# A diffusion trunk on one core: both panels' weights ahead of each modulation chunk, the last chunk directly behind the third on TensorE, and the high part ahead of silu in tile 0

## The reference

```python
def rms_norm(x, g):
    y = x * lax.rsqrt(jnp.mean(x * x, axis=-1, keepdims=True) + RMS_EPS)
    return y * g

def modulate(h, shift, scale):
    return h * (1.0 + scale) + shift

def swiglu(h, w_gu, w_down):                      # D_FF = 2816
    u = h @ w_gu
    return (jax.nn.silu(u[..., :D_FF]) * u[..., D_FF:]) @ w_down

for i in range(DEPTH):                            # DEPTH = 2, N_MOD = 9
    mx = (jax.nn.silu(c) @ ada_w[i] + ada_b[i]).reshape(B, 1, N_MOD, D_MODEL)
    mc = (jax.nn.silu(c_ctx) @ ada_w[i] + ada_b[i]).reshape(N_MOD, D_MODEL)
    x = x + 0.5 * mx[:, :, 2] * swiglu(modulate(rms_norm(x, norm_g[i, 0]), mx[:, :, 0], mx[:, :, 1]),
                                       ffn_w_gu[i, 0], ffn_w_down[i, 0])
    ...                                           # the same for ctx with mc
    # then a mixer (pooling and attention in layer 0, a recurrent block in layer 1), then a second swiglu
```

## Time and profile before

| | |
|---|---|
| median of 3 runs | 2848.53 us (2847.98 to 2848.59) |
| the profiled execution | 2844.29 us, span 2842.5 us |
| PE busy | 2685.2 us (94% of the span) |
| PE weight load busy | 2498.1 us (88%) |
| DVE, POOL, ACT busy | 1461.2, 905.6, 784.8 us |
| mean clock granted to PE | 0.975 of full |
| HBM read | 252.70 MB, 90 GB/s over the span |

### The profile page before, as it was taken

How to read it: one execution, slowest core, us unless ns; L and a number is a source line. 1 busy time by engine, 2 the same in 40 slices (tenths; PEclk the granted TensorE clock), 3 DMA queues, 4 the chain that set the end, 5 groups by cost and what they waited for, 6 DMA issues and landing times.

```text
span 2842.5 us, 40073 instructions
## 1 busy us (share of the span) xinstructions
PE 2685.2 (94%) x15151; PEld 2498.1 (88%) x15151; DVE 1461.2 (51%) x2479; ACT 784.8 (28%) x1053; POOL 905.6 (32%) x367
## 2 busy tenths in 40 slices
PE   6899999999989899999999999999998886899998
PEld 4899999998957899999998999999997775778887
DVE  5565456565363656556657324322248886432233
ACT  3222122222164322111122221111125664332222
POOL 0422233222322232322232232232324443344442
PEclk9999999999999999999999999999999998999999
DMA  5444344423300244434442223322211112233332
GB/s 202 119 118 132 97 118 118 132 75 79 108 27 27 70 118 118 137 93 118 118 136 57 59 59 96 89 61 64 68 46 52 56 52 58 68 94 99 89 104 80
DMA packets 413089, 256.87 MB, mean 90 GB/s; under 512 B 6653, under 2 KB 405846, under 8 KB 413014
## 3 DMA queue, kind: packets, MB, share of 16 engines
q1 hardware_dynamic: 413014, 255.87, 31.2%
HBM read 252.70 MB, written 4.25 MB: 90 GB/s over the span
## 4 chain that ended last, share of the span: by engine, by line
PE 51%; issue 29%; DVE 8%; POOL 7%; ACT 4%; DMA 0%; POOLq 0%; SPq 0%; DVEq 0%; ACTq 0%
PE pair_b L1696 24%; PE pair_a L1696 22%; POOL w_lo L711 7%; DVE ada_sums L1127 1%; DVE decay L1656 1%; DVE decay L1654 1%; DVE h_lo L1278 1%; DVE gate_i L1650 1%; DVE root L1648 1%; ACT decay L1065 1%; ACT root L1067 1%; PE pair_r L2051 1%; PE pair_c L2033 1%; PE pair_c L1778 1%; PE pair_a L1686 0%
## 5 line engine op out<-in xcount | busy, mean ns | idle before, releaser
L711 POOL TENSOR_TENSOR w_lo<-raw,w_hi 128x1024 fp32r<-128x1024 f32 (+3 forms) x302 | 837.4, 2774 | 1733.4 <-ACT w_hi L821 1733.4
L821 ACT ACTIVATE w_hi<-raw 128x1024 fp32r<-128x1024 f32 (+3 forms) x302 | 337.6, 1118 | 1279.3 <-PE pair_b L1696 440.6
L1167 DVE TENSOR_TENSOR work_g<-work_s,pair_b 128x768 f32<-128x768 f32 (+1 forms) x88 | 78.1, 888 | 680.9 <-PE pair_b L1696 518.2
L1127 DVE SCALAR_TENSOR_TENSOR ada_sums<-ada_raw,cvec,ada_sums 128x256 f32<-128x256 f32 x896 | 404.5, 524 | 0.0
L1696 PE MATMUL pair_a<-h_hi,w_hi 128*128 128x384 f32 x1312 | 340.6, 340 | 17.6 <-POOL w_lo L711 17.4
L1696 PE MATMUL pair_a<-h_lo,w_hi 128*128 128x384 f32 x1312 | 335.1, 336 | 0.0
L1696 PE MATMUL pair_a<-h_hi,w_lo 128*128 128x384 f32 x1312 | 334.4, 335 | 0.0
L1696 PE MATMUL pair_b<-h_hi,w_hi 128*128 128x384 f32 x1168 | 298.3, 336 | 8.4 <-POOL w_lo L711 8.4
L1696 PE MATMUL pair_b<-h_hi,w_lo 128*128 128x384 f32 x1168 | 297.5, 335 | 0.0
L1696 PE MATMUL pair_b<-h_lo,w_hi 128*128 128x384 f32 x1168 | 297.3, 335 | 0.0
L1696 PEld LDWEIGHTS pair_a<-h_hi,w_hi 128*128 128x128 f32 x1312 | 234.6, 189 | 30.0 <-issue 16.3
(11 more groups left out here) (290 smaller groups left out, 4330.7 us busy)
## 6 DMA issues: line engine op xcount, KB each, us to landing
raw<-in_ffn_w_gu_dram SPq DMA_DIRECT2D x176, 512.0 KB, 4.0
ada_raw<-in_ada_w_dram SPq DMA_DIRECT2D x64, 1024.0 KB, 5.2
raw<-in_ffn_w_down_dram SPq DMA_DIRECT2D x64, 704.0 KB, 5.5
raw<-in_rg_w_in_dram SPq DMA_DIRECT2D x20, 512.0 KB, 3.7
ada_first<-in_ada_w_dram SPq DMA_DIRECT2D x4, 2048.0 KB, 13.5
raw<-in_ab_w_in_dram SPq DMA_DIRECT2D x16, 512.0 KB, 3.9
raw<-in_rg_w_out_dram SPq DMA_DIRECT2D x8, 640.0 KB, 4.4
raw<-in_ab_w_out_dram SPq DMA_DIRECT2D x8, 512.0 KB, 4.1
```

What stands on the lines that cost most here:

```text
L711: nc.gpsimd.tensor_tensor(wl[:, par, 0:kt * P], raw[:, par, 0:kt * P], wh[:, par, 0:kt * P].bitcast(F32), ALU.subtract).then_inc(split_rea ...
L821: nc.scalar.activation(wh[:, par, 0:kt * P], raw[:, par, 0:kt * P], ACT.Copy).then_inc(hi_done, 1)
L1127: step = nc.vector.scalar_tensor_tensor(out=sums[v], in0=tiles(k), scalar=c_k, in1=sums[v], op0=ALU.mult, op1=ALU.add)
L1167: nc.vector.tensor_tensor(gbuf[:, 0, 0:W], sbuf[:, 0, 0:W], up, ALU.mult)\
```

## The change

Three edits. First, SP issues the loads of both panels of a tile, or of a pair of down panels, and the modulation chunk behind them. Second, PE runs `ada_rows(1)` directly behind `turn_ada(2)`, ahead of the first tile, and `turn_ada(3)` behind the first of the eight pieces. Third, in tile 0 of gu00 ACT rounds the next even panel before it takes silu; for this the tile is taken out of the loop.

```diff
                     def gate_up(i, between):
                         load(i * 2 + p0, 0, KD, gu[:, :, span(i * P + h * KC * P, P)])
+                        load(i * 2 + (p0 + 1), 1, KD, gu[:, :, span(i * P + (DFF + h * KC * P), P)])
                         between()
-                        load(i * 2 + (p0 + 1), 1, KD, gu[:, :, span(i * P + (DFF + h * KC * P), P)])
...
                         for r in range(2):
                             load(i * 2 + (p0 + r), r, KC, dn[:, h * KC:(h + 1) * KC, span(i * (2 * P) + r * P, P)])
-                            if r == 0:
-                                between()
+                        between()
...
                 p0, F0 = first[f"gu{f}{h}"], GU_BEFORE[f, h]
-                with act.Fori(0, KC - 1) as i:
+                if p0 == 0:
+
+                    for r in range(2):
+                        act.wait_ge(panel_used, r + 1)
+                        high(2 + r)
+                        if r == 0:
+                            silu(F0, p0)
+                with act.Fori(int(p0 == 0), KC - 1) as i:
                     silu(i + F0, i * 2 + p0)
...
             turn_ada(2, KD + 4)
+            ada_rows(1, pC[:, 512:1024])
 
             def modulation_ends(k0, half, r):
 
-                if (k0, half, r) == (0, 0, 1):
-                    ada_rows(1, pC[:, 512:1024])
-                elif (k0, half, r) == (0, 1, 0):
+                if (k0, half, r) == (0, 0, 0):
                     turn_ada(3, 4).then_inc(ada_used, 1)
```

## The result

The changed kernel takes **2823.51 us** (median of 4 runs, 2822.25 to 2825.37) against 2848.56 us for the kernel before (median of 4, 2847.98 to 2849.76). The ratio is 0.9912 with a 95% interval of 0.9895 to 0.9929.

A forecast was written before the change was run, and what follows sets the result against it. PE, busy 94% of the span, was taken as the bound, with gains from its idle time and the lower clock behind it. 5.3 + 0 + 4.9 + 2.9 + 4.8 = 17.9 us, so 2848.53 - 17.9 = 2830.6 us; range 2824 to 2838.

The forecast's parts named there:

- The last chunk and the opening: Ahead of tile 0 of gu00: the moved chunk makes the turn begin earlier, winning 5.3 us (4.1 to 7.1).
- The stop in tile 1 stays: Ahead of `pair_a` in gu00: POOL gets in behind all 14 sums, so PE still stands for 5.2 us.
- High part ahead of silu: Tile 0 of gu00: the earlier low-part request still falls into DVE's sums, so 0 us.
- The three stops of `pair_b`: gu00 tile 2, gu01 tile 1, gu10 tile 2: stops and slow stretches go, 4.9, 2.9 and 4.8 us.
- The median of the runs is 4.2 us above that execution: Whole kernel: the gain of 17.9 us taken off the median 2848.53 instead of the profiled 2844.29, giving 2830.6 us.
- POOL didn't get in earlier at tile 1: Rival at gu00 tile 1: low part let in behind the one running sum, 6.1 us more, 2824.5 us; 9%.
- The clock didn't take the opening back: Rival at gu00 tile 1: PE restarts at the lower clock and the 5.3 us are gone, 2836.1 us; 14%.
- No steady tile got a new stop: Slower rival: odd low part held by the sums, PE stands 2.5 us in each tile, 2930.6 us; 5%.

The follow-up runs named there:

- the high part first alone: Kernel before with only the third edit, tile 0 of gu00 out of the loop and rounding ahead of silu: 2847.9 us, ratio 1.0008.
- the panels two ahead: Changed kernel; DVE's sums wait for low parts (gu00, gu10), rounding before silu also in gu10, gu20, panels of tiles 1, 2 ahead of chunks 1, 2: 2819.26 us.

## Why the prediction missed its range

By its own steps:

- *The last chunk and the opening, 5.3 us:* right. In the pair of profiles it was 6.0. Over six profiles without the second edit the first product of gu00 starts at 75.2 us in the mean (73.6 to 76.5), over five with it at 70.0 (68.5 to 71.2): 5.2. Inside the term, the chunk took 3.64 us instead of 2.79 and began 0.5 us earlier than named, so two errors nearly cancel. The working itself gave 6.2 us. The 5.3 was chosen between 4.1 and 6.2, whose middle is 5.15, and that it meets the mean of 5.2 is luck.
- *The stop in tile 1 stays, with POOL held to the last sum:* right. PE started 2.25 us behind the end of the sums (71.82 against 63.94 + 5.63), and stood for 5.02 us where 5.2 were named.
- *High part ahead of silu, 0 us:* right beside the others. Alone, the ratio of 1.0008 can't be told from nothing, but the profile shows what the working left out: a table load less moves POOL's next request, and with the old order of the loads the stop in tile 2 becomes 1.9 us longer.
- *The three stops of `pair_b`, 12.6 us:* they went, in all five profiles of kernels with the first edit. The size was a little low. One profile was read, and it had the cheapest set of stops, if by little. The mean is 13.9 (1.3 more), and the three profiles of before spread from 12.3 to 14.8. The uncertainty was put at "one or two stretches at the lower clock more or less, 1.9 us each", in both directions; it should have been tilted towards more, since at 381 there was no such stretch, and another execution could only have had more of it.
- *"The median of the runs is 4.2 us above that execution, so against it 2848.53 - 17.9":* **this is the step that failed.** It carries the distance between one execution of before and its median over to a kernel that has no such distance: the two profiled executions of the changed kernel lie 0 and 1.5 us above its median. Against the profiled execution the sum gave 2826.4, which is 2.9 us from the result, and the pair of profiles bears out the sum to 0.2 to 0.4 us. Of the 7.1 us that the forecast lacks, 4.2 are this step, 2.7 came in that pair of executions where nothing was changed, and 0.2 are in the sum. A part of the 4.2 is the median that it starts from: it came from three runs, and of three later series of before two have a median 2.5 us lower. Against 2846.05 the change gives 22.5 us, and the forecast lacks 4.6. Before's runs lie between 2842.3 and 2855.4, with medians of 2846.0 to 2848.6, the changed kernel's eight between 2822.3 and 2825.4. That the upper ones of before's runs owe their length to slow stretches behind the stops, which the change takes away with them, fits the table above. So does a stop that grows by 3 us when POOL gets in among the sums, as at gu10 in the profile with the high part first alone. The runs without a profile can't show which of the two it was, or whether it was either.

The rivals: POOL didn't get in earlier at tile 1, although the time came out near that rival's 2824.5; it is the wrong reason for a nearly right number. The clock didn't take the opening back. No steady tile got a new stop.

What stays open: the profiles account for 5.2 us at the first product, 0.2 in tile 1 and 13.9 at the stops, 19.3 us in all. The medians show 22.5 (2846.05 against 2823.57) and 25.0. Of the 3 to 6 us between, 1.6 come and go with one slow stretch near 2480 us, which was there in all three profiles of before, absent in the changed kernel's first profile and there again in its second. The rest lies in executions that weren't profiled. The mean granted clock of their records is 0.974 over 36 runs of before and 0.976 over the changed kernel's eight, which fits slow stretches as the cause and doesn't show where they are.

## What to carry to other kernels

Price a stop of TensorE by its idle time and the slow stretch behind it, and read the second from several executions of the kernel before: one profile gives a draw. Don't carry the distance between a profiled execution and the median over to the changed kernel when the change removes what makes executions differ. In a queue that is served in order, ask of each load what it waits for; one that waits for a slow consumer delays all behind it, and a stop that is removed upstream can come back there. Taking an instruction off an engine that has time to spare isn't without effect either: it moves what that engine asks of others.

## What the runs showed of the hardware

- GpSimd held by a chain of VectorE operations isn't always held to its end. At 65.94 it was, amid 14 sums. At 84.40 it had asked 0.5 us behind the start of 14 sums, took its 2.59 us, and it was the sums that grew, from 5.63 to 7.77 us. In the fourteen profiles together, it got in each time that it asked between 0.2 us ahead of the start of 14 sums and 0.8 us behind it, and the sums took 7.76 us or more. At 1.8 us it got in 3 times of 19, each time in gu10, and from 2.0 us on never. Where it is there first, VectorE waits too. In the kernel with the panels two ahead, DVE's two operations that take 0.61 us elsewhere, and POOL's row beside them:

```profile
69.46 2.77 DVE L1139 TENSOR_SCALAR ada_sums<-ada_raw,cvec 128x256 f32<-128x256 f32 x2
```

```profile
69.68 2.41 POOL L720 TENSOR_TENSOR w_lo<-raw,w_hi 128x1024 fp32r<-128x1024 f32 x1 [0.71 <-ACT w_hi L830]
```

- 16 matmuls of `ada_rows` took 1.92 us at 51.75, and 3.64 at 0.50 in the stretch 43 to 49 above. The 2.79 at 31.14 was no price for the lower level, since its first 0.9 us ran at full clock. Two stretches of the kernel before, in the columns used above:

```profile
31.10:32.00 0.90, 0.90 (x10) 0.31 (x13) 0.44 (x3) 0.21 (x1) 0.90 (x1) 1.00 1.05 387
...
51.80:53.70 1.90, 1.90 (x18) 0.46 (x17) 0.00 (x0) 0.00 (x0) 0.00 (x0) 1.00 0.00 0
```

- The same stop of 2.5 us, at the same place, was followed by matmuls at the granted clock 1.00 in one execution and by a stretch with 0.86 in the mean in another.
- ACT's silu at 82.57 in the changed kernel has no table load ahead of it, where each tile of the kernel before paid 1.28 us (89.02 and 129.07). On an engine that waits 5 to 14 us a tile for PE the 1.28 us win no time by themselves. What they did was to move POOL's request in tile 1, and with it who waits for whom.
